# Chunked delta-rule scan: 32x32 transposes on VectorE, a two-instruction lower matrix, and an interleaved last level

## The reference, cut to what matters

```
m = where(strict, (k*beta) @ k.T * decay, 0)        # per chunk and head, strictly lower
t_inv = triangular_solve(eye + m, eye)              # unit lower triangular inverse
u, w = t_inv @ (v*beta), t_inv @ (k*beta*exp(g))
# then, chunk after chunk:
v_new = u - w @ state
o     = (q*exp(g)) @ state + a_intra @ v_new
state = state*exp(g_last) + k_dec.T @ v_new
```

## Time and profile before

| what | us |
|---|---|
| median of 3 runs (lowest, highest) | 3341.02 (3339.88, 3352.08) |
| span of the profiled execution | 3342.7 |
| TensorE busy (matmuls) | 3068.3, 92% |
| VectorE busy | 1791.6, 54% |
| ScalarE busy | 1278.8, 38% |
| GpSimd busy | 544.5, 16% |

### The profile page before, as it was taken

One profiled execution on the slowest core, in us unless ns is written; L12 is line 12 of the kernel. 1 busy time (PEld: TensorE's weight loads), 2 busy tenths in 40 slices (PEclk: granted clock), 3 DMA queues, 4 the chain that ended last, 5 costly groups with the idle time before them and its releaser, 6 DMA issues. The chain is left out here.

```text
span 3342.7 us, 60695 instructions
## 1 busy us (share of the span) xinstructions
PE 3068.3 (92%) x23542; PEld 2555.0 (76%) x23542; DVE 1791.6 (54%) x3171; ACT 1278.8 (38%) x2660; POOL 544.5 (16%) x475
## 2 busy tenths in 40 slices
PE   7997998797999998969939999999999989979799
PEld 6886997676999995648738888878888857758687
DVE  5655442264555544655475577565676545543433
ACT  5222333253444436841052323342323357720132
POOL 0000000242322330023203232242232200000000
PEclk9998999896999998979959999999999989989899
DMA  3213763342434334136463322353223262154543
GB/s 134 94 64 109 251 228 128 94 155 95 136 132 136 119 106 142 37 109 207 145 219 116 101 70 80 109 189 101 98 67 101 91 197 62 33 189 176 188 145 119
DMA packets 289637, 423.64 MB, mean 127 GB/s; under 512 B 41569, under 2 KB 178785, under 8 KB 284257
## 3 DMA queue, kind: packets, MB, share of 16 engines
q1 hardware_dynamic: 238784, 379.68, 34.0%
q10 hardware_dynamic: 50592, 40.38, 3.8%
HBM read 270.56 MB, written 149.42 MB: 126 GB/s over the span
## 5 line engine op out<-in xcount | busy, mean ns | idle before, releaser
L113 PE MATMUL pj_pp<-h_hi,pj_whi 128*128 128x512 f32 x1152 | 449.9, 391 | 5.8 <-POOL h_lo L2891 5.6
L114 PE MATMUL pj_pp<-h_lo,pj_whi 128*128 128x512 f32 x1152 | 448.9, 390 | 0.0
L115 PE MATMUL pj_pp<-h_hi,pj_wlo 128*128 128x512 f32 x1152 | 448.7, 390 | 0.0
L113 PEld LDWEIGHTS pj_pp<-h_hi,pj_whi 128*128 128x128 f32 x1152 | 216.6, 188 | 51.9 <-issue 7.0
L115 PEld LDWEIGHTS pj_pp<-h_hi,pj_wlo 128*128 128x128 f32 x1152 | 216.7, 188 | 45.1
L114 PEld LDWEIGHTS pj_pp<-h_lo,pj_whi 128*128 128x128 f32 x1152 | 216.7, 188 | 44.4
L2718 ACT CAST pj_whi<-w_raw 128x512 fp32r<-128x512 f32 x192 | 119.2, 622 | 327.5 <-PE pj_pp L115 318.5
L2782 DVE TENSOR_TENSOR pj_wlo<-w_raw,pj_whi 128x512 fp32r<-128x512 f32 x192 | 160.4, 836 | 12.4 <-ACT pj_whi L2718 9.4
L1099 DVE COPY_PREDICATED ds_z<-ds_zmask,ds_ps 128x128 f32<-128x128 int32 x160 | 47.0, 301 | 196.7 <-PE ds_ps L1328 196.7
L113 PE MATMUL np_pp<-h_hi,np_whi 128*128 128x512 f32 x384 | 150.2, 391 | 0.0
L115 PE MATMUL np_pp<-h_hi,np_wlo 128*128 128x512 f32 x384 | 149.5, 389 | 0.0
(11 more groups left out here) (346 smaller groups left out, 7575.7 us busy)
## 6 DMA issues: line engine op xcount, KB each, us to landing
w_raw<-in_w_second SPq DMA_DIRECT2D x192, 256.0 KB, 2.7
ds_pk<-scratch_pack SPq DMA_DIRECT2D x32, 1280.0 KB, 7.8
scratch_pack<-rp_out SPq DMA_DIRECT2D x32, 512.0 KB, 2.7
scratch_sig_fm<-pj_ob SPq DMA_DIRECT2D x64, 256.0 KB, 2.1
mb_sg<-scratch_sig_fm SPq DMA_DIRECT2D x16, 1024.0 KB, 7.7
rp_fm<-scratch_qkv_fm SPq DMA_DIRECT2D x96, 128.0 KB, 2.9
scratch_qkv_fm<-np_acc SPq DMA_DIRECT2D x11, 1024.0 KB, 4.8
np_acc<-in_x SPq DMA_DIRECT2D x16, 512.0 KB, 4.4
```

Of the source, the lines that this page charges most:

```text
L113: nc.tensor.matmul(out, ah, bh, start=(first and i == 0), stop=False)
L114: nc.tensor.matmul(out, ah, bl, start=False, stop=False)
L115: mm = nc.tensor.matmul(out, al, bh, start=False, stop=(last and i == n - 1))
```

## The change

Four edits inside `delta_scan`:

1. The transposes of levels 1 to 4 and that of `t1` leave TensorE. VectorE's `transpose`, which turns each 32x32 block in place of its own, writes `tt` from `u` (`turn`) and `u` from `t1` (`first_turn`). Up to level 4 the blocks that matter are no larger than 32x32. ScalarE's copies of the turned matrices go (`copy_u1`, and `copy_t` but for the last level's). The last level's 64x64 turn stays on TensorE.
2. `u` gets a second buffer, taken in turn by tile, so that the next tile's first turn can be written while the current one is in use.
3. `lower` becomes two instructions over all four heads: `kk*dec`, then, after a wait for the first, times the broadcast column of `ga`.
4. `last_y` and `last_x` alternate the two directions head by head, and wait at their start for both directions.

In VectorE's order `turn` of a level stands directly before that level's `fill`, direction by direction; `first_turn` stands directly after `first_level`.

```diff
-        u = [c.sb(f"u{d}", [P, 4, HP]) for d in D]
+        u = [[c.sb(f"u{d}{b}", [P, 4, HP]) for b in B] for d in D]
...
-                for h in range(4):
-                    ins = nc.vector.scalar_tensor_tensor(out=neg_m[d][b][:, h, :], in0=kk[d][:, cols[h]],
-                                                         scalar=ga[d][:, G_NBETA, h:h + 1],
-                                                         in1=dec[d][:, h, :], op0=ALU.mult, op1=ALU.mult)
-                ins.then_inc(m_done[d], 1)
+                nc.vector.tensor_tensor(neg_m[d][b][:], heads(kk[d][:]), dec[d][:], ALU.mult).then_inc(mk_done[d], 1)
+                dve.wait_ge(mk_done[d], i + 1 + START)
+                nc.vector.tensor_tensor(neg_m[d][b][:], neg_m[d][b][:],
+                                        ga[d][:, G_NBETA, :].unsqueeze(2).to_broadcast([P, 4, P]),
+                                        ALU.mult).then_inc(m_done[d], 1)
...
+            def first_turn(k, b, d):
+                dve.wait_ge(t1_done[d], k + 1 + START)
+                nc.vector.transpose(u[d][b][:], t1[d][:]).then_inc(u1_done[d], 1)
+
+            def turn(k, b, n, d):
+                dve.wait_ge(u_copied[d], k * NL + n + START)
+                nc.vector.transpose(tt[d][:], u[d][b][:]).then_inc(tt_done[d], 1)
...
                         for d in D:
+                            if n > 0:
+                                turn(i + 1, 1 - b, n, d)
                             fill(i + 1, n, d)
...
                             first_level(i + 2, b, 0)
+                            first_turn(i + 2, b, 0)
...
-                    if more and n > 0:
-                        for d in D:
-                            copy_t(i + 1, n, d)
...
-                if n > 0:
-                    for h in range(4):
-                        for g in B:
-                            mm = turn(d, u[d], g, h)
-                    mm.then_inc(t_turned[d], 1)
...
+            def last_y(k, b):
+                for d in D:
+                    pe.wait_ge(u_copied[d], k * NL + NL + START)
                 for h in range(4):
-                    mm = nc.tensor.matmul(ps[d][near, 0, h * HP:(h + 1) * HP], neg_m[d][b][far, h, near],
-                                          u[d][far, h, :], start=True, stop=True)
-                mm.then_inc(yx_done[d], 1)
+                    for d in D:
+                        near, far = at_half[d], at_half[1 - d]
+                        mm = nc.tensor.matmul(ps[d][near, 0, h * HP:(h + 1) * HP], neg_m[d][b][far, h, near],
+                                              u[d][b][far, h, :], start=True, stop=True)
+                        if h == 3:
+                            mm.then_inc(yx_done[d], 1)
...
+            def last_x(k):
+                for d in D:
+                    pe.wait_ge(yx_copied[d], k + 1 + START)
+                    pe.wait_ge(t_copied[d], k + 1 + START)
...
                 query_new(i, b, 0)
-                if more > 1:
-                    for d in D:
-                        turn_u1(i + 2, d)
                 query_new(i, b, 1)
```

More of the change, by code:

```diff
@@ L1151, in step @@
                     first_level(i + 2, b, 1)
+                    first_turn(i + 2, b, 1)
                 next_state(i, b, 1)
@@ L1167, in _ @@
                 first_level(0, 0, d)
+                first_turn(0, 0, d)
             for n in range(NL):
                 for d in D:
+                    if n > 0:
+                        turn(0, 0, n, d)
                     fill(0, n, d)
@@ L1174, in _ @@
             for d in D:
-                last_level(0, d)
+                last_level(0, 0, d)
                 first_level(1, 1, d)
+                first_turn(1, 1, d)
             steps(step)
@@ L1197, in row_exponent, with copy_t, copy_u @@
                 nc.scalar.activation(erow[d][b][:], ps[d][:, 3, :], ACT.Exp).then_inc(erow_done[d], 1)
[L1199 to L1207, removed]
-                turned = ps[d][rows, 1, 0:4 * HP].rearrange("p (h t) -> p h t", h=4)
[L1209 to L1214, removed]
+            def copy_t(k, d):
+                act.wait_ge(t_turned[d], k + 1 + START)
+                rows = at_half[d]
+                turned = ps[d][rows, 1, 0:4 * HP].rearrange("p (h t) -> p h t", h=4)
+                nc.scalar.copy(half(tt[d][rows], LEVELS[NL], d), half(turned, LEVELS[NL], d)).then_inc(t_copied[d], 1)
+            def copy_u(k, b, n, d):
                 act.wait_ge(u_done[d], k * NL + n + 1 + START)
-                nc.scalar.copy(half(u[d][:], LEVELS[n + 1], 1 - d),
+                nc.scalar.copy(half(u[d][b][:], LEVELS[n + 1], 1 - d),
                                packed(ps[d][:, 0, 4 * QP:8 * QP], LEVELS[n + 1])).then_inc(u_copied[d], 1)
@@ L1309, in row @@
                 mm.then_inc(row_done[d], 1)
[L1311 to L1317, removed]
-                for h in range(4):
-                    for g in B:
-                        mm = turn(d, t1[d], g, h)
-                mm.then_inc(u1_turned[d], 1)
-            def level_y(k, b, n, d):
-                pe.wait_ge(u_copied[d], k * (NL + 1) + n + 1 + START)
+            def level_y(k, b, n, d):
+                if n == 0:
+                    pe.wait_ge(u1_done[d], k + 1 + START)
+                    pe.wait_ge(x_copied[d], k + START)
+                else:
+                    pe.wait_ge(u_copied[d], k * NL + n + START)
                 for h in range(4):
@@ L1429, in step @@
                 if more:
-                    for d in D:
-                        last_y(i + 1, 1 - b, d)
+                    last_y(i + 1, 1 - b)
                 query_state(i, b, 1, more)
@@ L1434, in step @@
                 if more:
-                    for d in D:
-                        last_x(i + 1, d)
+                    last_x(i + 1)
                 query_new(i, b, 0)
-                if more > 1:
-                    for d in D:
-                        turn_u1(i + 2, d)
                 query_new(i, b, 1)
@@ L1446, in _ @@
             pe.wait_ge(preset, 2 * (3 + NL) + START)
-            for d in D:
-                turn_u1(0, d)
             for n in range(NL):
@@ L1457, in _ @@
                     level_u(0, n, d)
-            for d in D:
-                last_y(0, 0, d)
-            for d in D:
-                last_x(0, d)
-            for d in D:
-                turn_u1(1, d)
+            last_y(0, 0)
+            last_x(0)
             steps(step)
```

58 lines of the change are left out of this document (25 added, 33 removed).

## The result

| | before | after |
|---|---|---|
| median of the runs, us | 3340.5 (3338.7 to 3352.1, 4 runs) | 3295.6 (3276.0 to 3303.1, 4 runs) |
| profiled execution: span, us | 3342.7 | 3301.2 (own time 3303.1) |
| ratio of the runs | | 0.9855, 95% interval 0.9819 to 0.9891 |

The kernel is faster by 1.45%, 45 us. The forecast was 3265 us with a range of 3246 to 3292, so it promised 30 us more than came. The profiled execution of the changed kernel was the slowest of its four.

What follows compares the result with a forecast made beforehand. TensorE, busy throughout each step, was taken as the bound, then the pack load. Savings of 65 us in 14 steps, 4 in step 14 and 7 ahead made 76, so 3265 us, range 3246 to 3292.

Steps and rivals of the forecast that it cites:

- level to level: TensorE's time from one level's product to the next in a step, without turns there: near 3.1 us.
- its wait for both directions: At the step's end, `last_y` now waits for both directions' copies: +0.48 us a step.
- the turn: VectorE's transpose of 128x256, which no row showed: taken as 0.42 us, hidden in levels 1 to 3.
- the second lower matrix: Direction 1's lower matrix on VectorE as two wide instructions, running alone: 1.4 us, +0.3.
- the first 3.3: Direction 0's lower matrix on VectorE as two wide instructions beside GpSimd: 3.3 us, -1.1.
- The pack's wait: `differences(1)` waits for `a_t` after the pack load, delaying level 4's product to +14.4 us instead of +13.4.
- A step without stalls: Length of one scan step after the change, the pack's wait included, before adding stalls: 24.5 us.
- The 0.4 us a step added for stalls: Of TensorE's 0.6 us of stalls a step, 0.4 was kept, making the step 24.9 us.
- The alternating last level: `last_y` and `last_x` with directions alternating on TensorE: -0.54 and -0.43 us a step, against +0.48 for the wait.
- the last rival: TensorE's stalls or a lower granted clock eat the gain: about 3335 us, chance 0.03.
- the sum of 3266.7: Forecast span of the profiled execution: 3342.7 us less 76 us saved in the scan and its start.
- the start's -5.3 in place of -7: Ahead of the steps, tile 0's inversion at the 1.2 GHz level was to save 7 us of turns.

Runs made afterwards that it cites:

- e4: The changed kernel with only its turns on VectorE, lower matrix and last level as in the kernel before: 3288.8 us, ratio 0.9837.
- e12: The changed kernel with the last level's directions one behind the other, turns and wide lower matrix kept: 3296.9 us, ratio 0.9868.
- e9: The changed kernel with a second buffer for the decays, taken in turn by tile, run again on another chip: 3273.6 us, ratio 0.9797.
- e15: The kernel before with eight unused ScalarE copies ahead of level 3's u copies, so TensorE waits some 3 us a step: 3429.8 us, ratio 1.0237.
- e8b: The kernel before with four unused ScalarE copies ahead of level 3's u copies, so level 4's product waits: 3369.8 us, ratio 1.0072.
- e14: The kernel before with three unused ScalarE copies each ahead of the u copies of levels 0, 3 and 4: 3363.5 us, ratio 1.0044.

## Why the prediction was wrong

**The mechanism was right, and most sizes too.** Forecast and measured in a step at 2.4 GHz: level to level 3.1 and 3.09 us; `last_y` 0.93 and 0.91; its wait for both directions 0.48 and 0.46; the turn 0.42 and 0.44; the second lower matrix 1.4 and 1.4, the first 3.3 and 2.3. The Trainium skill ("VectorE: DVE Perf Modes", The three transpose paths) led to an estimate of 0.44 us for the turn: the trace agrees. The pack's wait is there and has its cause as told: ScalarE's `differences` waits for `a_t`. But it came twice. In the step shown it is direction 0's, whose `a_t` starts at +8.4 us and not +7.1 after the step's start (here, as in the prediction, level 0's product, 1029.29), and level 3's product waits 1.25 us; in three other steps it is direction 1's and level 4's product waits 0.79 to 0.94 us, as forecast. In the step shown level 4's product starts at +14.8 instead of +14.4.

**Small misses in the step:** `last_x` waits for VectorE, 0.3 us in the step shown and up to 0.9. Together with the pack's wait, which costs 0.4 more than forecast, it makes most of the difference. The copies L1117 take 1.54 us beside GpSimd and 0.59 alone; the prediction had priced only the turns and the lower matrix there. A step without stalls was forecast at 24.5 us and takes 25.28: 11 us over the 14 steps. The 0.4 us a step added for stalls, 5.6 us, were 3.8.

**A term that earns nothing by itself.** The alternating last level was forecast at 0.5 us a step net; e4 and e12 show none that can be measured.

**The step that failed** is the last rival, *it doesn't do what it says: TensorE's stalls or a lower granted clock eat the gain*, with a chance of 0.03 and the sentence against it "the new step keeps it busy for over nine tenths, and the dense step has 1.00". The new step does keep TensorE busy for 23.28 of 25.28 us, and the clock was 0.91 all the same. Busy share was the wrong thing to ask: e9 has less of it and 0.99. What decides is the length of single waits, and of those the prediction itself had found one of 1 us. It priced that wait at its own length and the clock at nothing. In the changed kernel's profile the steps take 34 us more than forecast: 11 for the longer step, 2 less for stalls, and 26 for 73.5 us at 1.2 GHz, 14 of them in the first step. The five profiles with VectorE's turns and one decay buffer give the same price: their scans, 396.6 to 421.0 us, follow the time at 1.2 GHz in them, 36.8 to 107.7 us, by 0.35 us for each (correlation 0.96), from 381 us with none. With the 34 us the sum of 3266.7 becomes the 3301.2 measured; the start's -5.3 in place of -7 and the 1.6 us less behind the scan cancel. Half of those 26 us is luck: the first step ran at 1.2 GHz in four of the eleven profiles with VectorE's turns. So for the median the clock is about 18 us, 3295.6 against the 3277 at before's clock, and the 12 from there to the forecast are about what the longer step costs.

How sure this is: that the clock carries the loss is shown by the step lengths, by the scans against the time at 1.2 GHz, and by e15 on the other kernel; the runs' mean clock alone would not show it, as before's runs vary with it too. That the wait for `a_t` causes 17 of 25 falls is shown by the second decay buffer, which takes that wait away and those falls with it, and gains 15 to 21 us, of which some 0.4 us a step, 6 us, is the wait itself. Not shown is why, of waits of the same length at the same place, some let the clock fall and some don't: ahead of level 4's product 6 of the thirteen waits of 0.86 to 0.97 us did with VectorE's turns, and none of the thirteen of 0.98 us in e8b; e14, meant to test waits near each other, brought no second wait about. Nor is it shown why the issue stalls grow as the step gets shorter.

## What to carry to other kernels

When a change makes the busiest engine wait where it never did, price each new wait twice: its length, and the stretch at the lower clock that a wait of about a microsecond may bring and one of over 1.5 us brought every time. Look first for the buffer behind the wait: doubling the decays' buffer took the wait away and gave 15 to 21 us, while matmuls put in to keep the engine busy gave nothing and cost 16 us once waits were short. Where an engine stalls and no releaser is named, look when the last instruction load ended among the DMA queues. And judge a variant whose clock varies by its runs and by the time at the lower clock, not by the number of falls in one profile.

## What the runs showed of the hardware

- VectorE's turn of 128x256 in 32-bit blocks takes 0.44 us (0.42 to 0.45 over 128 of them), beside GpSimd as well. A pair of copies of 64x256 from SBUF to SBUF, also with one input, takes 0.59 us alone and 1.54 beside GpSimd (1.04 at most for one); the Trainium skill ("GPSIMD Engine Reference", section 1 Specifications) tells that GpSimd collides with VectorE instructions that have two SBUF inputs or run in a two-port mode, and these two rows, each with one input, agree with it if the copy runs in such a mode and the turn doesn't. Here they are:

```profile
L1105 DVE STREAM_TRANSPOSE ds_tt<-ds_u x128: 420/437/446, 778.7 to 1202.2; 128x256 f32<-128x256 f32 x128
```
```profile
L1117 DVE COPY ds_uf<-ds_u x64: 242/291/1040, 797.2 to 1208.3; 64x256 f32<-64x256 f32 x64
```

- It goes both ways: two GpSimd multiplications of `qg` take 3.40 us beside the wide lower matrix, where they took 2.54 in the earlier trace rows.
- TensorE's granted clock fell to 1.2 GHz after single waits of about 1 us in a scan that was busy for over nine tenths, and came back after 3 to 24 us. Whether it falls after such a wait differs between executions of one kernel; after idle stretches of over 1.5 us it fell 20 times in 20 (11 of them in e15), after those of 0.8 to 1.0 us 10 times in 53.
- TensorE's stalls without a releaser, 62 of 0.4 to 2.6 us in 17 profiles, each end 1.20 to 1.62 us after the end of a 16 KB instruction load on queue q8.
